# Shortlist of 60 sums, inverses that grow in the accumulation banks, and other orders between stages, in a two-block transformer kernel

## What is computed

```python
# expert choice: 8 heads, two halves of 128 keys, 16 of each
v1, i1 = lax.top_k(s1, PEER_TOPK)
v2, i2 = lax.top_k(s2, PEER_TOPK)
cand_s = (v1[..., :, None] + v2[..., None, :]).reshape(TOKEN_CHUNK, PEER_HEADS, -1)
cand_i = (i1[..., :, None] * N_KEYS + i2[..., None, :]).reshape(TOKEN_CHUNK, PEER_HEADS, -1)
top_s, pos = lax.top_k(cand_s, PEER_TOPK)
e = jnp.take_along_axis(cand_i, pos, axis=-1)
...
# recurrent heads: the scan over tokens
sa = jnp.einsum('bhvk,bhk->bhv', state, a_t)
state = (state * w_t[:, :, None, :] + sa[..., None] * b_t[:, :, None, :]
         + v_t[..., None] * k_t[:, :, None, :])
y_t = jnp.einsum('bhvk,bhk->bhv', state, r_t)
```

## Time and profile before

| | |
|---|---|
| median of 3 runs | 3186.16 us (3182.36 to 3189.15) |
| profiled execution | 3181.46 us, of which span of the core 3179.6 us |
| PE busy | 2786.2 us, 88% of the span |
| DVE busy | 2287.3 us, 72% |
| ACT, POOL busy | 1275.4 and 804.8 us |
| mean granted TensorE clock | 0.923 |

### The profile page before, as it was taken

One profiled execution on the slowest core, in us unless ns is written; L12 is line 12 of the kernel. 1 busy time (PEld: TensorE's weight loads), 2 busy tenths in 40 slices (PEclk: granted clock), 3 DMA queues, 4 the chain that ended last, 5 costly groups with the idle time before them and its releaser, 6 DMA issues. The chain is left out here.

```text
span 3179.6 us, 55322 instructions
## 1 busy us (share of the span) xinstructions
PE 2786.2 (88%) x21767; PEld 1763.9 (55%) x21979; DVE 2287.3 (72%) x4103; ACT 1275.4 (40%) x2115; POOL 804.8 (25%) x471
## 2 busy tenths in 40 slices
PE   8887997977999999999798999678788766969998
PEld 4444455555677777777545566356666653434444
DVE  5795279997888888888763577577888861557752
ACT  4334243467333333333321477444545432333321
POOL 0760464500555554555401322000000001000000
PEclk9658998989999999999898999789999988989999
DMA  3003643567999999999532321311111004613321
GB/s 137 27 1 132 220 154 128 165 242 275 393 373 360 368 358 364 364 356 362 165 92 85 96 65 37 116 33 33 46 42 33 21 21 146 235 54 106 106 100 47
DMA packets 277533, 513.44 MB, mean 161 GB/s; under 512 B 19232, under 2 KB 166304, under 8 KB 275168
## 3 DMA queue, kind: packets, MB, share of 16 engines
q1 hardware_dynamic: 240480, 376.58, 34.8%
q0 software_dynamic: 36864, 134.23, 10.8%
HBM read 445.15 MB, written 65.60 MB: 161 GB/s over the span
## 5 line engine op out<-in xcount | busy, mean ns | idle before, releaser
L1717 PE MATMUL banks<-gated_hi,v_hi 128*128 128x384 bf16 (+2 forms) x1536 | 335.0, 273 | 0.0
L1717 PE MATMUL banks<-gated_lo,v_hi 128*128 128x384 bf16 (+2 forms) x1536 | 335.0, 273 | 0.0
L1717 PE MATMUL banks<-gated_hi,v_lo 128*128 128x384 bf16 (+2 forms) x1536 | 335.0, 273 | 0.0
L1555 POOL DMA_INDIRECT gathered_u<-in_u_rows,first_tile_rows x128 | 212.4, 1660 | 305.6 <-DVE gathered_dots L1663 156.1
L1560 POOL DMA_INDIRECT gathered_v<-in_v,first_tile_rows x128 | 175.4, 1370 | 201.9 <-DVE x_tokens L1655 182.1
L1717 PEld LDWEIGHTS banks<-gated_hi,v_hi 128*128 128x128 bf16 x1536 | 150.3, 98 | 55.5
L1704 PE MATMUL banks<-act_hi,u_hi 128*128 128x384 bf16 x512 | 168.0, 328 | 12.0 <-DVE u_lo L1641 12.0
L2297 POOL TENSOR_TENSOR gates_w<-branch_raw,gates_w 128x1024 bf16<-128x1024 f32 x8 | 17.1, 2136 | 603.2 <-ACT gates_w L2587 603.2
L1116 PE MATMUL banks<-act_hi,early_u_hi 128*128 128x384 bf16 x512 | 168.9, 330 | 0.0
L1116 PE MATMUL banks<-act_lo,early_u_hi 128*128 128x384 bf16 x512 | 168.6, 329 | 0.0
L1655 DVE SCALAR_TENSOR_TENSOR x_tokens<-gathered_v,gathered_weights,x_tokens 128x1024 f32<-128x1024 f32 x128 | 164.0, 1282 | 6.1 <-issue 1.8
(11 more groups left out here) (585 smaller groups left out, 7711.5 us busy)
## 6 DMA issues: line engine op xcount, KB each, us to landing
shared_room<-in_u SPq DMA_DIRECT2D x128, 512.0 KB, 3.8
shared_hi<-in_v SPq DMA_DIRECT2D x64, 512.0 KB
shared_lo<-in_v SPq DMA_DIRECT2D x64, 512.0 KB
gate_tables<-gate_piece SPq DMA_DIRECT2D x12, 2048.0 KB, 8.6
gate_group<-gate_tables SPq DMA_DIRECT2D x32, 768.0 KB
late_raw<-in_ffn_up SPq DMA_DIRECT2D x22, 1024.0 KB, 6.9
early_gelu<-early_gelu_columns SPq DMA_DIRECT2D x64, 192.0 KB, 1.8
gelu_early_rows<-early_gelu SPq DMA_DIRECT2D x32, 384.0 KB
```

The lines of the kernel that those rows point to most:

```text
L1555: pool.indirect_dma_start(gu[:, n % GROUP, :], None, u_table, bass.IndirectOffsetOnAxis(ap=rows.index[:, 0, n:n + 1], axis=0)).then_inc(gu ...
L1717: m = pe.matmul(ps[:, bank, to:to + width], v[:, j, cols], w[:, j, tok:tok + width], start=start and n == 0 and to == 0, stop=stop and n = ...
```

## The change

- `pick_experts` compares 60 instead of 256 pair sums per head: pair (a, b) of sorted lists can be among the best 16 only if (a+1)(b+1) is at most 16, and `PIECES` covers those pairs by four rectangles. Position to key numbers goes by 15 small operations on 128 elements, and compare, multiply and tree of additions are done on bf16.
- `rwkv_heads` is rewritten: X and its transpose live in banks 1 to 4; PE adds X·(L·X) onto the bank itself (`start=False`), so the sum with X and the masked copy are gone. One product L·X serves both orientations (both heads in bank 0). The masks are now products with bf16 masks. Small products of one 128 x 512 result go one after another through bank 7 (`SMALL`), the chain through bank 6, gates through 5. POOL does five products of the preparation (`kp`, `rk`, `ones_rk`, `kt`, `rt`), one copy of the identity and six zero memsets of `RQ` (128 x 2048 bf16) per turn. Gate products are 48 ahead of the turns and 42 a turn. The group norm of pair i-2 ends in turn i (it was i-1).
- `PostBetween` runs ACT's and DVE's parts of two tiles interleaved, and PE's first transpose lies before the last bank of w_out. `AfterExperts` and `FirstNorm` make the low parts of their first weights on DVE, in another order, and PE starts a first bank on half of the weight. Norms load ACT's square root table ahead (`table`). `nsa_projection` multiplies a chunk that feeds compression before the 48 columns of gate logits. `GateParts` starts earlier and stores while it splits. The load of x (2 MB) moves from the end of `rwkv_heads` to between the branch weights and the gain rows of `branches_to_end`, ahead of `in_w_out`.

The core of the diff:

```diff
-                    link(dve.tensor_tensor(cand[:].rearrange("p h (a b) -> p h a b", b=TOPK),
...
+                    for at0, a0, a1, width in PIECES:
+                        n = a1 - a0
+                        ins = dve.tensor_tensor(cand[:, :, at0:at0 + n * width].rearrange("p h (a b) -> p h a b", b=width),
...
+PIECES = ((0, 0, 1, 16), (16, 1, 3, 8), (32, 3, 8, 4), (52, 8, 16, 1))
+CANDIDATES = 60
...
-                    for f, buf in ((0, cand), (1, cand2)):
-                        hit = buf[:].rearrange("p h (a b) -> p (h a) b", b=TOPK)
...
+                        hit = hits[:, f].rearrange("p h j (k two) -> p (h j) k two", two=2)
+                        ins = dve.tensor_tensor(hit, hit, idx16[:, f].unsqueeze(2).to_broadcast([P, PH * TOPK, TOPK // 2, 2]),
+                                                ALU.mult)
...
+                    n = TOPK // 2
+                    while n > 1:
+                        for f in range(2):
+                            ins = dve.tensor_tensor(hits[:, f, :, 0:n, :], hits[:, f, :, 0:n, :], hits[:, f, :, n:2 * n, :], ALU.add)
...
+                def xlx(i, s):
+                    b, slot = 1 << s, i % 2
+                    xt = xt_at(slot)
+                    steps.wait("invert", "vector", i, f"between{s}")
+                    for h in range(2):
+                        for m in range(NCH):
+                            cols = slice(m * P, (m + 1) * P)
+                            if s < STAGES - 1:
+                                bank = ps[:, bank_x(h, slot), cols].rearrange("p (n two b) -> p n two b", two=2, b=b)[:, :, 0, :]
+                                for one, other in passes(lambda l: W3[:, h, l, xt, m, :],
+                                                         lambda l: blocks(RQ[:, s % 2, h, l], b, 0)[:, m]):
+                                    pe.matmul(bank, one, other, start=False, stop=True, skip_group_check=True)
...
+DENSE_BEGIN = 48
+DENSE_AT = [6] + [3] * 12
+LAST_PASSES = 16
...
-        return {1: range(0, 2), 2: range(2, 8), 3: range(8, self.count)}.get(c, ())
+        return {1: range(0, 6), 3: range(6, 8), 4: range(8, 12), 5: range(12, self.count)}.get(c, ())
...
+        def again(t):
+            act.wait_ge(post.added, 2 * t + 2)
+            norm.square(act, t)
+            norm.root(act, t)
...
+        second_half(0)
+        second_half(1)
+        again(0)
+        second_half(2)
+        again(1)
+        norm.high(act, 0)
```

More of the change, by code:

```diff
@@ L552, in scalar @@
         norm = self.norm
+        norm.table(act)
         for t in range(NT):
@@ L613, in tensor @@
             bank(t)
-        if self.norm is not None:
-            for t in range(NT):
-                self.norm.turn(pe, t)
-class StoreTail(PostBetween):
-    def __init__(self, k, post):
-        super().__init__(post, None)
-        self.k = k
-        self.stored = k.sem("result_stored")
     def sync(self, sp):
@@ L663, in pool @@
     def pool(self, pool):
-        for q in range(QS):
-            self.first.low(pool, q)
+        pool.memset(self.k.ones1[:], 1.0).then_inc(self.one_set, 1)
     def scalar(self, act, first):
@@ L700, in tensor @@
         norm.turn(pe, 0)
-        norm.turn(pe, 1)
-        weights_split()
+        pe.wait_ge(self.first.low_done, QS // 2)
         for t in range(NT):
@@ L2435, in chain @@
+                def chain(j, part):
                     c, what = divmod(part, 3)
@@ L2486, in low_part, with add_bonus, gated @@
+                def add_bonus(j):
+                    end(dve.tensor_tensor(o[:], o[:], bon3[:, j % 3, :], ALU.add), hold=True)
+                def gated(j):
+                    steps.wait("rest", "scalar", j, "gate")
+                    end(dve.tensor_tensor(o[:], o[:], gate3[:, j % 3, :], ALU.mult), "out")
                 def low_part(j):
                     steps.wait("finish", "scalar", j, "out_hi")
-                    end(dve.tensor_tensor(ol[:, bass.ds(j, 1), :], one(o), oh[:, bass.ds(j, 1), :], ALU.subtract), "out_lo", hold=True)
@@ L2540, in _, with finish @@
+                def finish(j):
+                    centre(j)
+                    variance(j)
+                    over_deviation(j)
+                    affine(j)
+                    add_bonus(j)
+                    gated(j)
+                    low_part(j)
+                chain(KD - 1, 0)
+                finish(KD - 2)
+                for part in range(1, 3 * NCH):
+                    chain(KD - 1, part)
+                finish(KD - 1)
             @block.scalar
@@ L2638, in chain @@
+                        invert(act.copy(out, bank), f"grown{s}{h}")
                 def chain(j, part):
@@ L2731, in _ @@
+                for part in range(3 * NCH):
+                    chain(KD - 1, part)
+                    if part == 0:
+                        finish(KD - 2)
+                    outs(part)
+                finish(KD - 1)
             @block.tensor
@@ new lines, in norm, with gram @@
+                def norm(j):
+                    steps.wait("first", "scalar", j, "kk2")
+                    steps.wait("first", "scalar", j, "rate")
+                    steps.wait("rest", "scalar", j - 1, "tok0")
+                    for c in range(NCH):
+                        ins = pe.matmul(ps[:, SMALL, 2 * c:2 * c + 2], kk2[:, c * P:(c + 1) * P], ones_h[:, 0:P:HD],
+                                        start=True, stop=True)
+                    first(ins, "norm")
+                def gram(j, g, h):
+                    left, right = ((kt, at2), (bt, rt2), (kt, rt2))[g]
+                    rows = slice(h * HD, (h + 1) * HD)
+                    for c in range(NCH):
+                        cols = slice(c * P, (c + 1) * P)
+                        ins = pe.matmul(ps[:, SMALL, cols], left[rows, cols], right[rows, j % 2, cols], start=True, stop=True)
+                    rest(ins, f"gram{g}{'ab'[h]}")
@@ L2824, in chain @@
-                def chain(j, slot, part):
+                        steps.wait("invert", "vector", i, f"grown{s - 1}{h}" if s > 1 else f"x0{h}")
+                        for m in range(NCH):
+                            to = (h * NCH + m) * HALF
+                            out = ps[:, BETWEEN, to:to + HALF].rearrange("p (n b) -> p n b", b=b)
+                            for n, (one, other) in enumerate(passes(lambda l: left[:, h, l, m, :],
+                                                                    lambda l: blocks(W3[:, h, l, 1], b, 0)[:, m])):
+                                ins = pe.matmul(out, one, other, start=n == 0, stop=n == 2)
@@ L2936 @@
+                for part in range(3 * NCH):
+                    chain(KD - 1, part)
+                    dense(LAST_PASSES)
+                    if part == 1:
+                        turn_y(KD - 2)
+                turn_y(KD - 1)
 CAUSAL_FIRST = 12
-DENSE_FIRST = 12
-DENSE_PASSES = 3
-LAST_PASSES = 16
 def dense_bank(p):
```

1517 lines of the change are left out of this document (883 added, 634 removed).

## The result

The changed kernel takes 3048.74 us (median of 4 runs, 3045.99 to 3054.95), before 3185.55 (3182.36 to 3189.15): ratio 0.957, 95% interval 0.956 to 0.959. The forecast was 2991 with a range of 2940 to 3055, so the time lies in the range near its slow end. Most of the gain that is missing was lost in one stage.

The account below looks back on a forecast made before the run. The prediction took DVE to bound the choice of experts and a loop of hand-offs the recurrent heads; terms summing to -192.6 us took 3181.5 to 2988.9, set at 2991 on the median's scale, range 2940 to 3055.

Parts of the forecast that it names:

- rival (a): Recurrent heads: turns of 62 to 72 us through bank 7's hand-offs and POOL's products, 3030 to 3105 us; chance 0.22.
- Heads: Recurrent heads: the chain of hand-offs decides, 57 us a turn where the trace has 70; -126 us.
- the last turn 62: Recurrent heads: last turn goes from 79 to 62 us, with 192 passes at 0.216 making 41.4 of it.
- PE falls to about 45: Recurrent heads: PE's work in a turn falls from 54.7 to about 45 us.
- POOL gets 31 us: Recurrent heads: POOL, idle before, gets 31 us a turn, with six memsets at 3.6 and products at some 1.4.
- the walk that gave 57: Recurrent heads: start and six levels priced step by step, 54.7 us, plus two for DVE and POOL collisions.
- Choice of experts: Choice of experts: DVE falls from 57.2 to 42 to 48 us per tile, PE becomes the bound; -31 us.
- Query product: Query product: a wait and a tail go, six splits ahead of a cast cost 8.5 us; -1, bounds -5 and +5.
- Join and order: Join of the blocks: -10 us by low parts on DVE and half the weight; sparse attention's input chunk order: -9.5.
- PostBetween: Between w_out and feed-forward: norms done under banks of w_out shorten PE's waits for L233; -17 us, -12 to -19.
- Load of x: Behind the recurrent heads: 2 MB, hidden before, now go ahead of in_w_out on the critical chain; +5.4 us.
- Start: Start of the kernel: -3.5 us of PE's 6.8 us wait; then the second chunk's low part decides.

Follow-up runs that it names:

- experiment 5: Changed kernel with the 48 gate passes ahead of the turns moved into them (48 instead of 42 a turn), nothing left out: 3034.8 us.
- experiment 9: Changed kernel with the load of x behind the critical chunk of in_w_out and the first two branch weights loaded earlier: 3044.1 us.
- experiment 6: Changed kernel with POOL's five products in the recurrent heads replaced by memsets to zero, so POOL reads nothing: 3046.7 us.
- experiment 3: Changed kernel with POOL zeroing the low parts of early expert rows in the choice of experts instead of computing them: 3042.5 us.
- experiment 11: Changed kernel with the old tile-after-tile order of norms between w_out and the feed-forward product: 3072.0 us.
- experiments 2 and 8: Each from the changed kernel: the first with the old choice of experts, 3078.0 us; the second without the load of x, 3048.6 us.
- experiments 5 and 10: The second: changed kernel with the edits of experiment 5 and experiment 9, plus two instead of six gate splits ahead of the query weight's cast: 2992.5 us.
- experiment 4: Changed kernel with 9 of each 24 gate and branch passes, the other 15 and most low parts left out: 3042.2 us.

## Why the prediction was right, and where its terms failed

The time lies 6 us inside the slow end of the range, and the heads alone are 43.3 short of their forecast. The range was kept wide on that side for rival (a), and not for the clock that used up the room, so that part is luck.

**Heads: loop and bare turn right, the clock left out.** The prediction priced each pass at full speed and made a turn of 57; 57.8 was measured at clock 1.00. It took the clock for nothing, since before the change it was nothing: turns of 70 us at 0.98 and at 0.93. With that slack gone a turn stretches with the clock. The term is 5 x 57 + 50 + 54 = 389 us for seven turns, and it measured 416.8; length times (1 - clock) is 28, the 27.8 between them, though so close a match is chance (turn by turn it is off by up to 2.5). With the clock at 1.00 the first two turns took 50.0 and 56.5 in experiment 5, where 50 and 54 were forecast. Ahead of the first level 1.6 more were lost. A second failing step is "the last turn 62": it and the last inversion are late by what is left of the 43.3, some 14. Of that 5.1 is the clock (0.89 over 46.5 us) and 6.85 the branch weight's load, which the prediction did not follow to its tile and its place on SP; experiment 9 gave 4.4 of it back. Some 2 stay open.

"PE falls to about 45" was low: 49.6 at clock 1.00, and 54 with the clock lost. "POOL gets 31 us" was high: 19.4, since the 3.64 of the earlier trace rows are two memsets and the prediction read them as one; a memset over 2048 took 1.8. On DVE the items named take 57.8 to 48.5 only, the other 5.5 down to 43 being called smaller remains; 42.0 to 42.7 was measured. None of the three was a term of the sum. But the walk that gave 57 was made with such prices, so its total is better confirmed than its parts.

**Rival (a)** gave turns of 62 to 72 by two mechanisms. Turns of 62 to 65 did occur in profiled executions, by the clock. POOL's reads cost no time on the path (experiment 6). The single bank no run varied, and the trace does show it: these are PE's longest waits in the turn at clock 1.00, 2397.8 to 2455.6.

```profile
PE banks L3015 <- DVE shared_room L2537: 2.0, 1, 2.0
PE banks L3038 <- DVE grams_t L2574: 1.7, 1, 1.7
...
PE banks L3038 <- ACT kk_norms L2798: 1.0, 1, 1.0
PE banks L3011 <- ACT shared_room L2784: 0.9, 1, 0.9
```

Each stands ahead of a product into bank 7 and ends with an instruction that reads this bank. With two smaller ones (0.3 and 0.2) they make 6.1 us, of the 8.2 that PE is not busy, and 6 is what the rival had for them. The turn took 57.8 all the same. So this half of the rival's mechanism was there and did not lift the turn above the forecast; what more banks would give is not shown.

**Choice of experts: collisions mis-sized.** Direction, 60-wide searches (215 ns, interpolated 214) and the sum without collisions (40.2, forecast 41.5) held. What failed is "some collisions with POOL's split left I take 42 to 48": 51.8, since collisions cost 11.6 us a tile and not up to 6.5. The mean of 51.8 lies just under PE's 52.4, but PE still waited 10.9 us. The old operations over 2048 float32 elements were few and took 2.3 to 3.7 us each; the new ones are many and short, most with two operands in SBUF, and each may stand behind a POOL instruction of 2.13 us. The Trainium skill ("SBUF — State Buffer", Who interferes with whom) says a DVE instruction with two SBUF inputs contends with a POOL instruction that reads SBUF and not with one that only writes it. The trace agrees, with 1222 ns against 2181, for these two-input operations; experiment 3 has a cast that was held by a memset too. That makes the number of such instructions the thing to count.

**Query product: bounds right, value 4.9 off.** The cast came at 289.3, as forecast (280.1 plus some 8.5). But that moment is set by landings, and the stage itself had begun 5.6 earlier, at 251.6 instead of 257.2, by the start's gain; so the cast was 14.8 later in its stage, and the start's gain was lost there. The gains behind it were 10.7, about the 9.5 of the forecast (5.2 + 3 + 1.3). **Join and order: -15.0 for -19.5.** Chunk order gave 8.7 by its wait, the join 6: the start came 8.9 earlier relative to the end of `run_experts` (18.0 from 26.9 us), of which the rest was lost between tiles, in 4.1 us of PE's wait for `act_lo` and 5.8 for `nsa_out`. **PostBetween: -17 forecast, 18.9 by experiment 11. Load of x: +5.4 forecast, 5.1 by the landing, 5.7 by leaving it out, 5.3 by moving it. Start: -5.4 for -3.5.**

What stays open: why the clock falls in one turn and not in its twin. Eight of the profiled kernels have the same instructions in their turns, and their middle turns take from 57.7 to 65.2 us. It is not mere chance: the kernels of experiments 2 and 8 show the same seven lengths within 0.1 us (60.6, 60.3, 65.2, 64.7, 62.3 in the middle turns of the first), and so do those of experiments 5 and 10. No run varied what they may have in common.

## What to carry to other kernels

When a loop of hand-offs has slack, a fall of TensorE's clock can be free, and the profile before hides its price; a change that removes the slack pays it. Price the tightened loop at the mean granted clock of the trace, not at full speed, and fill PE's gaps inside the loop with work that has to be done anyway: it cost nothing here and brought 14 us, 3 of them ahead of the loop. Before one big vector operation is split into many short ones, count those with two SBUF operands beside a POOL that reads, and casts and tensor-scalar operations beside any POOL instruction. Where a row merges instructions (x2), divide before you price one. And if runs differ by the clock, read a term of 5 us in the trace's stage and not in the median.

## What was not expected of the hardware

The clock fell although PE was busy for most of the time. Windows of 6 us around one fall in the changed kernel:

```profile
2174.00:2180.00 6.00, 4.00 (x81) 3.30 (x80) 5.14 (x10) 1.74 (x5) 0.00 (x0) 1.00 0.01 3
2180.00:2186.00 6.00, 5.82 (x76) 5.19 (x74) 3.78 (x9) 4.10 (x10) 1.80 (x1) 1.00 0.01 3
2186.00:2192.00 6.00, 4.26 (x60) 3.76 (x60) 3.36 (x8) 1.99 (x5) 0.00 (x0) 0.86 0.00 0
2192.00:2198.00 6.00, 5.67 (x53) 4.67 (x52) 3.05 (x5) 1.45 (x4) 3.08 (x2) 0.57 0.00 0
2198.00:2204.00 6.00, 5.75 (x102) 5.14 (x101) 4.32 (x8) 2.65 (x6) 1.77 (x1) 1.00 0.60 167
```

PE is busy 4.0, 5.8 and 4.3 of 6 us and then runs for some us mostly at the lower of its two levels, 1.2 GHz, though it is busy 5.7 of 6 by then. Taking work off PE (experiment 4) brought more time at that level, and turns of up to 66.8 us. And the time of an operation on DVE depends on what POOL does beside it: one over 128 elements (L1382) took 291 ns at the least and 2245 at the most.
